# Two engines' written-out orders, GpSimd's share and one wait of TensorE, in the seven-product units of a decoder trunk

## The reference, cut to what matters

```python
u = rmsnorm(h, g_pre)
f = jnp.square(jax.nn.relu(u @ w_ff_in)) @ w_ff_out      # D_MODEL 1024, D_FF 4096
h = h + rmsnorm(f, g_post)
```

## Time and profile before

| | us |
|---|---|
| median of 3 runs | 1691.79 (1690.87 to 1695.0) |
| the profiled execution | 1694.92, its span 1693.0 |
| TensorE busy | 1586.5 (94% of the span) |
| VectorE busy | 956.5 (56%) |
| ScalarE busy | 737.4 (44%) |
| GpSimd busy | 213.4 (13%) |

### The profile page before, as it was taken

How to read it: one execution, slowest core, us unless ns; L and a number is a source line. 1 busy time by engine, 2 the same in 40 slices (tenths; PEclk the granted TensorE clock), 3 DMA queues, 4 the chain that set the end, 5 groups by cost and what they waited for, 6 DMA issues and landing times.

```text
span 1693.0 us, 31505 instructions
## 1 busy us (share of the span) xinstructions
PE 1586.5 (94%) x13500; PEld 1463.1 (86%) x13500; DVE 956.5 (56%) x1215; ACT 737.4 (44%) x1283; POOL 213.4 (13%) x206
## 2 busy tenths in 40 slices
PE   7999899988989899999999879999999799898998
PEld 7787699988989899999999555657999799898998
DVE  6888547665473646733342475652665745547472
ACT  5444655435252444522232367664452532525442
POOL 1000000012020210010240352210000211202100
PEclk9999999999999999999999899999999999999999
DMA  7533062313123152322246200003222132312321
GB/s 207 151 97 105 21 205 73 110 44 100 63 88 112 39 168 75 99 84 61 65 125 212 94 1 1 1 1 100 75 76 88 39 125 75 100 63 88 113 75 53
DMA packets 139768, 146.98 MB, mean 87 GB/s; under 512 B 6578, under 2 KB 131330, under 8 KB 139295
## 3 DMA queue, kind: packets, MB, share of 16 engines
q1 hardware_dynamic: 138351, 138.23, 25.9%
q0 software_dynamic: 1280, 6.75, 1.3%
HBM read 132.08 MB, written 10.87 MB: 84 GB/s over the span
## 4 chain that ended last, share of the span: by engine, by line
PE 81%; DVE 8%; ACT 5%; issue 4%; DMA 1%; SPq 1%; ACTq 0%; DVEq 0%
PE ps L408 44%; PE ps L800 5%; PE ps L802 4%; PE ps L801 4%; PE ps L541 3%; PE ps L1584 2%; PE ps L1431 2%; PE ps L1430 2%; PE ps L1432 2%; PE ps L2111 2%; PE ps L2089 1%; DVE w_lo L393 1%; PE ps L2090 1%; PE ps L2032 1%; PE ps L594 1%
## 5 line engine op out<-in xcount | busy, mean ns | idle before, releaser
L408 PE MATMUL ps<-hid_hi,w_hi 128*128 128x272 f32 x1280 | 268.8, 289 | 2.2 <-DVE hid_lo L2412 1.5
L408 PE MATMUL ps<-hid_hi,w_lo 128*128 128x272 f32 x1280 | 267.5, 288 | 0.0
L408 PE MATMUL ps<-hid_lo,w_hi 128*128 128x272 f32 x1280 | 266.6, 288 | 0.0
L393 DVE TENSOR_TENSOR w_lo<-w_raw,w_hi 128x2048 fp32r<-128x2048 f32 x71 | 165.0, 2324 | 123.0 <-ACT w_hi L388 121.0
L408 PE MATMUL ps<-x_hi,w_hi 128*128 128x272 f32 x896 | 201.5, 292 | 11.4 <-DVE x_lo L2951 4.3
L388 ACT ACTIVATE w_hi<-w_raw 128x2048 fp32r<-128x2048 f32 x71 | 135.4, 1907 | 174.8 <-PE ps L408 171.7
L408 PEld LDWEIGHTS ps<-hid_hi,w_hi 128*128 128x128 f32 x1280 | 202.0, 188 | 3.9 <-issue 2.3
L408 PEld LDWEIGHTS ps<-hid_lo,w_hi 128*128 128x128 f32 x1280 | 202.1, 189 | 0.0
L408 PEld LDWEIGHTS ps<-hid_hi,w_lo 128*128 128x128 f32 x1280 | 200.9, 189 | 0.0
L408 PE MATMUL ps<-x_hi,w_lo 128*128 128x272 f32 x896 | 198.9, 289 | 0.0
L408 PE MATMUL ps<-x_lo,w_hi 128*128 128x272 f32 x896 | 198.3, 288 | 0.0
(11 more groups left out here) (437 smaller groups left out, 3297.0 us busy)
## 6 DMA issues: line engine op xcount, KB each, us to landing
w_raw<-in_ffn_w_out SPq DMA_DIRECT2D x64, 512.0 KB, 4.4
w_raw<-in_ffn_w_in SPq DMA_DIRECT2D x58, 512.0 KB, 4.6
w_raw<-in_nsa_w_in SPq DMA_DIRECT2D x20, 512.0 KB, 4.5
w_raw<-in_ple_w_gate SPq DMA_DIRECT2D x16, 512.0 KB, 3.9
w_raw<-in_conv_w_in SPq DMA_DIRECT2D x15, 512.0 KB, 5.7
w_raw<-in_conv_w_out SPq DMA_DIRECT2D x8, 512.0 KB, 4.1
w_raw<-in_nsa_w_o SPq DMA_DIRECT2D x8, 512.0 KB, 4.5
conv_in_turned<-conv_in SPq DMA_DIRECT2D x16, 203.2 KB, 2.6
```

The lines of the kernel that those rows point to most:

```text
L393: dve.tensor_tensor(WL[par][:, :], RAW[par][:, :], WH[par][:, :].bitcast(F32), ALU.subtract)\
L408: m = pe.matmul(o_, w[par][:, wcols:wcols + P], x[:, k, c_], start=f, stop=l)
```

## The change

- `fast_pe`: product 2 waits for ScalarE's copy of product 0 alone.
- `quad_pool` and `fast_pool` go; `quad_dve` does the same subtraction on VectorE, and `fast_sums` gets a case "s1". GpSimd has nothing left in these units. The evictions' waits on `h_ready` go, since VectorE itself has read the content; s2 no longer makes VectorE wait for its own end, and s4 waits for it instead.
- `fast_act` and `fast_dve` become written-out lists.
- The entry is a list of its own, `fast_entry_dve`, in which the last two additions (quarters 2 and 3) or copies (quarter 1) into `F` stand between the pieces and s1 stands behind the second.

```diff
                     elif i == 2:
                         pe.wait_ge(S["g_act"], un + 1)
-                        pe.wait_ge(S["g_dve"], NC + 7 * un + 1)
...
-                L(dve.tensor_tensor(a_, z_, d_, ALU.add), S["g_sum"])
+                L(dve.tensor_tensor(a_, z_, d_, ALU.add), S["g_sum"], wait=False)
+            elif which == "s1":
+                L(dve.tensor_tensor(c_, c_, d_, ALU.add), S["g_s1"], wait=False)
...
-        def quad_pool(pool, L, l, q, u, n):
+        def quad_dve(dve, L, l, q, u, n):
...
+            dve.wait_ge(S["hid_hi"], h + 1)
+            L(dve.tensor_tensor(HL[:, rows, c], two(TMP[n][:, :]), HH[:, rows, c].bitcast(F32), ALU.subtract), S["h_ready"], wait=False)
...
-                dve.wait_ge(S["h_ready"], h - 3 + x if u or q > 1 else h)
...
+        def first_product(act, L, l, q, u):
+            un = UNITS * (3 * l + q - 1) + u
+            act.wait_ge(S["g_full"], NC + PRODS * un + 1)
+            act.wait_ge(S["h_ready"], 8 * (4 * l + q) + 4 * u - (3 if u or q > 1 else 0))
+            L(act.activation(two(TMP[0][:, :]), PS[:, 0:2, 0:HT], ACT.Copy), S["g_act"], wait=False)
...
+            # fast_act, second unit, from its third piece on
+            fast_hi(act, l, q, s0, b0, 1, 2)
+            fast_hi(act, l, q, s0, b0, 1, 3)
+            first_product(act, L, l, q, 1)
+            fast_hi(act, l, q, s0, b0, 1, 4)
+            quad_act(act, L, l, q, 0, 3)
+            fast_hi(act, l, q, s0, b0, 1, 5)
+            fast_hi(act, l, q, s0, b0, 1, 6)
+            quad_act(act, L, l, q, 1, 0)
...
+            # fast_dve, from the first unit's last eviction on
+            evict_dve(dve, L, l, q, 0, 6)
+            fast_lo(dve, L, l, q, s0, 1, 2)
+            fast_sums(dve, L, l, q, s0, 1, "s4")
+            fast_sums(dve, L, l, q, s0, 1, "s1")
+            fast_lo(dve, L, l, q, s0, 1, 3)
+            quad_dve(dve, L, l, q, 0, 2)
+            fast_lo(dve, L, l, q, s0, 1, 4)
+            evict_dve(dve, L, l, q, 1, 0)
+            fast_lo(dve, L, l, q, s0, 1, 5)
+            quad_dve(dve, L, l, q, 0, 3)
+            evict_dve(dve, L, l, q, 1, 1)
+            fast_lo(dve, L, l, q, s0, 1, 6)
+            evict_dve(dve, L, l, q, 1, 2)
+            quad_dve(dve, L, l, q, 1, 0)
+            evict_dve(dve, L, l, q, 1, 3)
+            evict_dve(dve, L, l, q, 1, 4)
+            first_half_lo(dve, L, l, q, s0)
+            evict_dve(dve, L, l, q, 1, 5)
+            second_half_lo(dve, l, q, s0)
+            quad_dve(dve, L, l, q, 1, 1)
+            evict_dve(dve, L, l, q, 1, 6)
+            quad_dve(dve, L, l, q, 1, 2)
+            quad_dve(dve, L, l, q, 1, 3)
...
+        def fast_entry_dve(dve, L, l, q, s0, evict):
+            fast_lo(dve, L, l, q, s0, 0, 0)
+            fast_sums(dve, L, l, q, s0, 0, "s3")
+            fast_sums(dve, L, l, q, s0, 0, "s2")
+            evict(0)
+            fast_lo(dve, L, l, q, s0, 0, 1)
+            fast_sums(dve, L, l, q, s0, 0, "s1")
+            evict(1)
...
-            fast_pool(pool, L, 1, S_FFN1)
...
-            fast_pool(pool, L, 0, S_FFN0)
```

More of the change, by code:

```diff
@@ L876, in fast_sums @@
                 dve.wait_ge(S["g_lo"], NC + n + 1)
-                L(dve.tensor_tensor(a_, z_, d_, ALU.add), S["g_sum"])
+                L(dve.tensor_tensor(a_, z_, d_, ALU.add), S["g_sum"], wait=False)
+            elif which == "s1":
+                L(dve.tensor_tensor(c_, c_, d_, ALU.add), S["g_s1"], wait=False)
             else:
                 dve.wait_ge(S["g_lo"], NC + n + 3)
+                dve.wait_ge(S["g_sum"], 3 * un + 2)
                 L(dve.tensor_tensor(b_, a_, b_, ALU.add), S["g_sum"], wait=False)
@@ L963, in evict_dve @@
                     L(dve.tensor_tensor(out, PS[:, 6:8, 0:HT], VACC[:, :, :], ALU.add), S["g_dve"], wait=False)
-        def fast_act(act, L, l, q, s0, b0):
[L967 to L983, removed]
+        def first_product(act, L, l, q, u):
[3 more added lines that the diff above has]
+            L(act.activation(two(TMP[0][:, :]), PS[:, 0:2, 0:HT], ACT.Copy), S["g_act"], wait=False)
@@ new lines, in fast_act @@
+        def fast_act(act, L, l, q, s0, b0):
+            fast_hi(act, l, q, s0, b0, 0, 2)
+            fast_hi(act, l, q, s0, b0, 0, 3)
+            first_product(act, L, l, q, 0)
+            fast_hi(act, l, q, s0, b0, 0, 4)
+            fast_hi(act, l, q, s0, b0, 0, 5)
+            fast_hi(act, l, q, s0, b0, 0, 6)
+            quad_act(act, L, l, q, 0, 0)
+            fast_hi(act, l, q, s0, b0, 1, 0)
+            quad_act(act, L, l, q, 0, 1)
+            fast_hi(act, l, q, s0, b0, 1, 1)
+            quad_act(act, L, l, q, 0, 2)
+            fast_hi(act, l, q, s0, b0, 1, 2)
[6 more added lines that the diff above has]
+            quad_act(act, L, l, q, 1, 0)
+            first_half_hi(act, l, q, s0)
+            quad_act(act, L, l, q, 1, 1)
+            second_half_hi(act, l, q, s0)
+            quad_act(act, L, l, q, 1, 2)
@@ L984, in fast_act @@
             quad_act(act, L, l, q, 1, 3)
         def fast_dve(dve, L, l, q, s0, b0):
[L988 to L1004, removed]
@@ L1005, in fast_dve @@
-            evict_dve(dve, L, l, q, 1, 6)
+            fast_lo(dve, L, l, q, s0, 0, 2)
+            fast_sums(dve, L, l, q, s0, 0, "s4")
+            fast_lo(dve, L, l, q, s0, 0, 3)
+            fast_lo(dve, L, l, q, s0, 0, 4)
+            evict_dve(dve, L, l, q, 0, 0)
+            fast_lo(dve, L, l, q, s0, 0, 5)
+            evict_dve(dve, L, l, q, 0, 1)
+            fast_lo(dve, L, l, q, s0, 0, 6)
+            evict_dve(dve, L, l, q, 0, 2)
+            quad_dve(dve, L, l, q, 0, 0)
+            fast_sums(dve, L, l, q, s0, 1, "s3")
@@ new lines, in fast_dve @@
+            evict_dve(dve, L, l, q, 0, 3)
+            evict_dve(dve, L, l, q, 0, 4)
+            fast_lo(dve, L, l, q, s0, 1, 0)
+            fast_sums(dve, L, l, q, s0, 1, "s2")
+            evict_dve(dve, L, l, q, 0, 5)
+            quad_dve(dve, L, l, q, 0, 1)
+            fast_lo(dve, L, l, q, s0, 1, 1)
+            evict_dve(dve, L, l, q, 0, 6)
[3 more added lines that the diff above has]
+            fast_lo(dve, L, l, q, s0, 1, 3)
@@ L1242, in ffn_dve, with first_out @@
                     turn_x_dve(dve, L, l, gain, j - 4)
+                def first_out(mb):
+                    c = 6 + mb
+                    dve.wait_ge(blk_full, b0 + 8 + c + 1)
+                    L.count[blk_free] = b0 + 8 + c
+                    L(dve.tensor_copy(two(F[:, c, :]), blk(mb)), blk_free)
+                if j == 7:
+                    fast_entry_dve(dve, L, l, 1, s0, first_out)
+                    continue
                 for mb in range(2):
@@ L1253, in ffn_dve @@
                         L(dve.tensor_copy(two(F[:, c, :]), blk(mb)), blk_free)
[L1254 to L1257, removed]
             for q in range(1, 4):
@@ L1260, in ffn_dve, with add_out @@
                 b_e, s_e = b0 + 8 + 8 * q, s0 + 4 + 4 * q
+                def add_out(c):
+                    dve.wait_ge(blk_full, b_e + c + 1)
+                    L.count[blk_free] = b_e + c
+                    L(dve.tensor_tensor(two(F[:, c, :]), blk(c % 2), two(F[:, c, :]), ALU.add), blk_free)
                 for j in range(4):
[L1262 to L1268, removed]
+                    if j == 3 and q < 3:
+                        fast_entry_dve(dve, L, l, q + 1, s0, lambda mb: add_out(6 + mb))
+                        continue
+                    split_lo(dve, s_e + j + 1, (s_e + j + 1) % 2)
                     if q == 3 and j:
@@ L1273, in ffn_dve @@
                     for mb in range(2):
[L1274 to L1277, removed]
+                        add_out(2 * j + mb)
                     if q == 3 and j == 2:
```

## The result

The changed kernel took 1629.7 us (median of 4 runs, 1628.92 to 1630.82), the kernel before, beside it, 1692.51 us (4 runs, 1690.87 to 1695.0). The ratio is 0.9628 (95% interval 0.9612 to 0.9645). The forecast was 1628, in a range from 1621 to 1642.

What follows compares the result with a forecast made beforehand. TensorE, busy 94%, bounds the kernel, so only its waits and slow products can be won: 38.0 + 8.1 + 2.6 + 0.7 + 13.0 + 1.3 = 63.7 us, from the median 1691.79 to 1628 us, range 1621 to 1642.

Steps and rivals of the forecast that it cites:

- The wait of product 2: Units of quarters 1 to 3: TensorE's 12 idle waits for VectorE's eviction 0 ahead of product 2 go, 38.0 us.
- not this wait: Rival at product 2: something other than eviction 0 holds it, only the entry's 10 us fall, 1681 us; chance 0.04.
- The slow products: Six second-unit products 2, slowed by the clock behind long waits, return from 31.12 us to full speed: 13.0 us.
- The entry: Each layer's entry into quarter 1: TensorE's four waits go, 8.1 us, and layer 1's slow product, 1.3 us.
- the walk: Hand-timed VectorE and ScalarE order through entry and second unit; narrowest spare 0.7 us at product 5, 0.6 us behind units.
- The lower ends: VectorE's taken-over work at its lowest cost, 0.72 us per subtraction and 1.22 us per s1; the forecast uses these.
- the upper ends: The taken-over work at GpSimd's cost, 1.43 and 2.34 us: product 5 and the outer part wait, 11 us, 1639.
- VectorE sets the pace: Rival: VectorE's 0.7 us is used up, second units' product 5 or the outer part waits, 1634 to 1645; chance 0.18.
- ScalarE's copy: Rival at product 2: it waits for ScalarE's copy of product 0, 4 us stay, 1632; within the 0.76 case.
- The slower rival: VectorE held 2.0 us before each subtraction by ScalarE's triple: 1704 us, slower from 1.7 us each; chance 0.02.
- The loads: SyncE's loads behind `fast_lo` land 4.4 us after issue, 5 and at least 1.5 us before need: they stay hidden.
- The rule: Skill's advice to move work off saturated VectorE, even to GpSimd, would mean 1639; forecast overrides it, 39.0 of 42.3 us.

Runs made afterwards that it cites:

- the first experiment: The kernel before with TensorE's wait for eviction 0 ahead of product 2 taken out, nothing else changed: 1660.45 us, ratio 0.9799.
- the runs with additions: The changed kernel with one or three unused 544-column VectorE additions ahead of eviction 2 in each second unit: 1625.63 us (one; again 1627.53), 1639.16 us (three).

## Why the prediction was right, point by point

*The wait of product 2 and its 38.0 us.* It was VectorE's eviction 0, as its end 0.10 us ahead of the matmul said, though the view of waits put it down to "issue". The rival "not this wait" (1681) is out by the first experiment alone, which took out nothing else.

*The slow products, 13.0 us.* 31.12 - 18.18 = 12.9. In each run a product behind a short pause kept its 3.0 us, and one behind a long pause mostly did not.

*The entry, 8.1 + 1.3 us.* No pause, and a granted clock of 1.00 from 205.8 to 919.2 us and from 967.0 to 1625.7, which takes in all units of both layers. VectorE in order of time at the entry of quarter 1, in the changed kernel:

```profile
345.42 1.21 DVE L863 TENSOR_TENSOR w_lo<-w_raw,w_hi 128x1024 fp32r<-128x1024 f32 x1
...
351.37 1.22 DVE L878 TENSOR_TENSOR w_raw<-w_raw 128x1024 f32<-128x1024 f32 x1
353.45 0.72 DVE L1285 COPY sub_out<-ps 128x544 f32<-128x544 f32 x1 [0.86 <-PE ps L408]
```

The first `fast_lo` starts 8.4 us earlier than in the earlier trace rows; s1 ends at 352.59 (the walk had 352.3), ahead of the last copy, which alone still waits for TensorE's block.

*The sum.* The profiled span fell by 1693.0 - 1628.6 = 64.4 us, where the terms make 63.7; the medians fell by 62.8. The two layers' quarters 1 to 3, each with the step into its first matmul, fell by 607.17 - 542.85 = 64.3 us, before and after:

```profile
sum 607.17, PE 561.09 PEld 556.97 DVE 337.01 ACT 244.50 POOL 99.14; mean PE 280.54 PEld 278.48 DVE 168.50 ACT 122.25 POOL 49.57
...
sum 542.85, PE 542.85 PEld 542.35 DVE 336.52 ACT 243.68 POOL 2.75; mean PE 271.43 PEld 271.17 DVE 168.26 ACT 121.84 POOL 1.37
```

So the whole gain lies where the prediction put it. A quarter fell from 99.46 to 90.38 us (90.5 was forecast).

*VectorE's new work.* The lower ends held, 0.72 and 1.22 us; the upper ends (1639) did not occur. "VectorE sets the pace" stayed away by 0.9 us at product 5, and the runs with additions show that it would have started there. *ScalarE's copy* was a wait in the old order without `g_dve` (0.51 us), and none in the new one. *The slower rival* would have needed 1.7 us of waiting in front of each subtraction; the 48 together waited 11.5 us, 0.24 each. *The loads* stayed hidden: no row of the waits names a DMA in the units.

*The rule.* VectorE's share of the stretch of a quarter's 14 products, third of the busy times:

```profile
444.53:486.81 42.28, 42.28 (x339) 42.28 (x338) 35.91 (x39) 28.39 (x37) 0.00 (x0) 1.00 0.28 88
```

It is 35.9 of 42.28 us, 85%. The prediction's 39.0 (92%) counts each instruction in full, though those back to back overlap by 0.08 us, and takes in three that run behind the units; the walk, which has the overlap, is not touched by that. VectorE was not what TensorE waited for, and giving GpSimd its share back changed nothing that could be measured in the time. The Trainium skill, "Perfetto Trace Analysis", section Optimizing Scalar/DVE Operations, says that work may be moved off a saturated VectorE, and that moving it between VectorE and GpSimd, which share a read port of SBUF, might not help; the second half agrees with the run that gave GpSimd its share back. By these runs the share of busy time did not decide, the spare time ahead of the next eviction did.

*What the prediction had not said* is how the gain divides. The wait alone is worth 34 us, the new order with GpSimd's withdrawal (wait kept) 1694.62 - 1665.45 = 29, both 63: here they add up, although each was thought to need the other. The reason can be read in the pauses: without the wait the old order still loses its time at product 3, at the outer parts and at the entry; with the wait the new order still loses it at product 2. GpSimd's withdrawal is worth 14 us for s1 alone in the old order with the wait, and no more than 0.9 us of the quarters in the new one without it; in the old order without the wait it was not run.

## What to carry to other kernels

When TensorE waits for an in-order engine, walk that engine's list from a fixed point, note for each result when it is ready and when it is wanted, and look at the smallest difference: here such a walk gave the ends of both narrow places within 0.3 us, where the busy share (92% in the prediction, 85% in the trace) pointed to a bound that was not there. A wait put down to "issue" still has a releaser; look for the instruction that ends a tenth of a us ahead, twice alike. The cost of two engines that collide depends on whether something is queued behind the one that is slowed: price a move between engines in the order in which it will run, not in the old one.

## What the runs showed of the hardware that was not expected

The clock's fall behind a pause of TensorE was not the same each time. Behind 5.48 us (before) and 3.86 us (only s1 moved) it fell at all six second units; behind 3.26 us (wait put back) at five of six; behind the entry's 2.67 us in the kernel before in layer 1 only, without the wait in both layers; behind pauses of 1.6 us or less in these units never. A fall made the product behind it, 24 matmuls, take up to 5.6 us in place of 3.0 (5.47 in the row above, behind 3.26 us of pause). Behind the five pauses of 3.26 us where it fell, the product took 1.5 to 2.5 us longer, so that such a pause cost 4.8 to 5.7 us. What else decides whether it falls, these runs do not show.

A two-input VectorE instruction of 544 columns took the same with one operand in PSUM (L943, 719 ns) as with both in SBUF (L930, 721 ns).
